# The first half of the latent branch moved ahead of the last pair's weighting

## The chip, the cores and the metric

One core of one Trainium2 chip. The metric is the device time of one launch in microseconds; lower is better. The program computes two transformer layers for 256 tokens, with weights that are read from HBM in each run.

## The reference, cut to what matters

Each layer runs three token mixers side by side on the same normalized input, projects each mixer's output to the model width, gates the three and adds them:

```python
y_a = einsum('bsk,kd->bsd', y_a, w_br_a)   # latent attention: 8 heads x 64 = 512 rows of weights
y_b = einsum('bsk,kd->bsd', y_b, w_br_b)   # block-sparse attention: 4 heads x 64 = 256 rows
y_c = einsum('bsk,kd->bsd', y_c, w_br_c)   # index-selected attention: 4 heads x 64 = 256 rows
g_a, g_b, g_c = split(sigmoid(gate_logits), 3)
merged = g_a * y_a + g_b * y_b + g_c * y_c
x = x + gate1 * (merged @ w_out)
...                                        # then SwiGLU, with its own norm
```

The projection of the latent attention (`y_a @ w_br_a`) is "the latent branch".

## The kernel before, in words

**Slabs.** All weights come as slabs of 128 partitions x up to 2048 words, numbered by their use, through a ring of three. For each slab SP issues a load into `raw` (it waits until the slab three before has been split), ACT rounds it into `w_hi` (`hi`, line 1006, which waits for the data and until TensorE has used the slab three before) and DVE subtracts for `w_lo` (`lo`, line 1377). TensorE then multiplies three times for each tile: hi x hi, hi x lo, lo x hi (`passes`, lines 543 to 545 in the helper's calls). `slab_used` counts the slabs that TensorE is done with.

**Attention.** Sixteen heads, in the order 4 of b, 8 of a (latent), 4 of c, run as a software pipeline that is written out by hand on each engine. On TensorE the loop `for n in range(NH + 4)` issues, per step, the scores of head n + 1, the transposes of head n - 3 (`turn_p`, line 819), every second step the weighting of a pair of heads (`weigh_v`, lines 837 and 841), and at eight of the steps half a slab of gate logits (`gate_slab`). The last steps are n = 18 (transposes of head 15, second half of gate slab 11) and n = 19 (`weigh_v(7)`, the last pair).

ACT copies the transposed weights out of PSUM (line 1271), then writes `y_hi` of a finished pair (line 1276, waits for `pv_done` of that pair). DVE writes `y_lo` of the pair (line 1708). `y_lo_done` counts the pairs; the latent heads are pairs 2 to 5, the c heads are pairs 6 and 7.

**After the attention.** For each half `hf` of the model width there are two slabs: `S_BR + 2 * hf` holds the latent branch (48 matmuls, "part a"), `S_BR + 2 * hf + 1` holds the b branch and the c branch (24 matmuls each, "part b" and "part c"). TensorE's order for half 0 is: part a (waits for `y_lo_done` of 6 pairs), eight transposes of a gate row (`turn_row`, line 575, wait for `gate_out`), part b, part c (waits for all 8 pairs). For half 1: part a (waits for the row copies, `row_out`), then a wait for `m_done` 2, part b, part c. Then the output projection `w_out`. Part b of half 1 writes the PSUM banks that DVE has to read for the merge of half 0; this is what `m_done` guards.

ACT's order there is: `y_hi` of pair 7, `hi` of slab `S_BR + 2`, `hi` of slab `S_BR + 3` (needs `slab_used` of `S_BR`, that is part a of half 0), two row copies (line 1055), `hi` of `S_OUT`, the rounding of the merged tiles (line 1296).

DVE's order there is: `lo` of `S_BR + 1`, `y_lo` of pair 7, `lo` of `S_BR + 2`, `lo` of `S_BR + 3`, then for half 0 two products of gate and latent branch (line 1734, need part a), two rounds of two products and two sums (lines 1745, 1749, 1750, need part c; the end of each round counts `m_done`), the low parts (line 1756), then `lo` of `S_OUT` and the same for half 1.

POOL waits for `pv_done` of the last pair before it issues the next three loads of adaLN weights (1 MB each) into buffers that the attention used.

Of the kernel before, what the change touches and what calls it, by code (L numbers as in the profile page):

```python
# [13 lines left out]
P = 128  # L14
D = 1024
T = 256
# [7 lines left out]
A_HEADS, A_NOPE, A_ROPE, A_QK, A_V = 8, 64, 32, 96, 64  # L24
Q_RANK, KV_RANK = 768, 256
B_HEADS = C_HEADS = 4
# [33 lines left out]
S_BR = S_GATE1 + 10  # L60
# [95 lines left out]
def gate_slab_no(g):  # L156

    return S_GATE0 + g if g < 2 else S_GATE1 + g - 2


def gate_bank(g):

    return 7 - g if g < 2 else (g + 1) % 3 if g < 6 else g - 5 if g < 8 else g % 2
# [18 lines left out]
NH = len(HEADS)  # L182
# [7 lines left out]
BR_BANKS = ((4, 6, 2), (0, 2, 4))  # L190
# [16 lines left out]
def build(nc, x, c, ada, slabs, vec, gain_rows, const, out):  # L207
    with ExitStack() as ctx:
        def sb(name, shape, dt=F32):
            return ctx.enter_context(nc.sbuf_tensor(name, shape, dt))  # L210

        def event(name, per_layer):
            return Event(ctx.enter_context(nc.semaphore(name)), per_layer)
# [8 lines left out]
        y_hi = sb("y_hi", [P, KT, T], F32R)  # L222
        y_lo = sb("y_lo", [P, KT, T], F32R)
# [83 lines left out]
        bank = [ctx.enter_context(nc.psum_tensor(f"bank{i}", [P, 512], F32)) for i in range(8)]  # L307
# [16 lines left out]
        slab_used = event("slab_used", NS)  # L324
# [27 lines left out]
        row_out = event("row_out", 4)  # L352
# [43 lines left out]
        y_lo_done = event("y_lo_done", NH // 2)  # L396
# [125 lines left out]
        def _(pe):  # L522
# [14 lines left out]
            def slab(l, s):  # L537
                pe.wait_ge(lo_ready.sem, lo_ready.at(l, s + 1))
                return (l * NS + s) % RING
# [7 lines left out]
            def channel_tile(slot, o, col, offs, act_hi, act_lo, opens, first, final):  # L547

                for n, off in enumerate(offs):
                    last = passes(o, w_hi[:, slot, off + col:off + col + P], w_lo[:, slot, off + col:off + col + P],  # L550
                                  act_hi[n], act_lo[n], first and opens and n == 0, final and n == len(offs) - 1)
                return last

            def channel_slab(slot, tiles, first, final):

                for o, col, offs, act_hi, act_lo, opens in tiles:
                    last = channel_tile(slot, o, col, offs, act_hi, act_lo, opens, first, final)
                return last
# [27 lines left out]
            def gate_slab(l, g, tiles=(0, 1)):  # L586

                s = gate_slab_no(g)
                slot = slab(l, s)
                if g >= 5:  # L590

                    pe.wait_ge(gate_out.sem, gate_out.at(l, g - 2 if g < 8 else g - 1))
                hi, lo = [h_hi[:, k, :] for k in range(KT)], [h_lo[:, k, :] for k in range(KT)]
                last = channel_slab(slot, [(bank[gate_bank(g)][:, m * T:(m + 1) * T], m * P,
                                            [256 * k for k in range(KT)], hi, lo, m == 0) for m in tiles], True, True)
                if 1 in tiles:
                    last.then_inc(slab_used.sem, 1)
# [20 lines left out]
            for l in range(DEPTH):  # L618
# [10 lines left out]
                if l == 0:  # L629
# [17 lines left out]
                    slot = (l * NS + S_A) % RING  # L647
# [51 lines left out]
                for k in range(KT):  # L699
                    slot = slab(l, S_B + k)  # L700
# [82 lines left out]
                for kind, src in ((0, q_a), (1, k_a)):  # L783
# [6 lines left out]
                    for h in range(A_HEADS):  # L790
                        for t in range(TT):
                            at = (h % 2) * T + t * P
                            m = (t * A_HEADS + h) * A_QK
# [4 lines left out]
                def scores(n):  # L798
                    kind, h = HEADS[n]
                    if kind == "a":  # L800
                        q, k = qk_t[0:A_QK, h, :], qk_t[0:A_QK, A_HEADS + h, :]
                    else:
                        j = (0 if kind == "c" else 1)
                        q, k = pq_t[:, 2 * j + h // 2, :], kz_t[:, 4 * j + h, :]
                    if n >= 2:

                        pe.wait_ge(ttr_done.sem, ttr_done.at(l, 2 * (n - 1)))
                    b = bank[4 + n % 2]
                    nc.tensor.matmul(b[:, 0:P], q[:, 0:P], k[:, 0:P], start=True, stop=True)
                    nc.tensor.matmul(b[:, P:P + T], q[:, P:T], k[:, :], start=True, stop=True).then_inc(scored.sem, 1)  # L810

                def turn_p(n):

                    pe.wait_ge(p_ready.sem, p_ready.at(l, n + 1))
                    if n >= 2:

                        pe.wait_ge(pt_out.sem, pt_out.at(l, n - 1))
                    for j in range(3):
                        last = nc.tensor.transpose(bank[6 + n % 2][:, j * P:(j + 1) * P],
                                                   p_sb[n % 5][:, j * P:(j + 1) * P], ident)  # L820
                    last.then_inc(p_tp.sem, 1)

                def weigh_v(pair):

                    if pair == 0:

                        pe.wait_ge(gate_out.sem, gate_out.at(l, 8))
                    if pair >= 2:

                        pe.wait_ge(y_lo_done.sem, y_lo_done.at(l, pair - 1))  # L830
                    pe.wait_ge(pt_out.sem, pt_out.at(l, 2 * pair + 2))
                    y, at = bank[2 + pair % 2], []
                    for n in (2 * pair, 2 * pair + 1):
                        kind, h = HEADS[n]
                        at.append({"a": P * h + A_NOPE, "b": C_BV + HD * h, "c": C_CV + HD * h}[kind])
                    for e in range(2):
                        nc.tensor.matmul(y[HD * e:HD * (e + 1), 0:T], proj[:, 0, at[e]:at[e] + HD],
                                         pt_sb[(2 * pair + e) % 3][:, 0:T], start=True, stop=False,
                                         skip_group_check=True)
                    for e in range(2):  # L840
                        nc.tensor.matmul(y[HD * e:HD * (e + 1), P:T], proj[:, 1, at[e]:at[e] + HD],
                                         pt_sb[(2 * pair + e) % 3][:, T:T + P], start=False, stop=True,
                                         skip_group_check=True).then_inc(pv_done.sem, 1)


                pe.wait_ge(mla_out_a.sem, mla_out_a.at(l, 4))
                scores(0)
# [3 lines left out]
                for n in range(NH + 4):  # L851
                    if 1 <= n < NH - 1:
                        scores(n + 1)
                    if 3 <= n <= NH + 2:
                        turn_p(n - 3)
                    if n >= 5 and n % 2:
                        weigh_v((n - 5) // 2)
                    if n in GATE_STEPS:
                        half = GATE_STEPS.index(n)
                        gate_slab(l, 8 + half // 2, (half % 2,))  # L860

                for hf in range(2):
                    banks = BR_BANKS[hf]

                    def branch(slot, b0, base, k0, n_k):
                        hi, lo = [y_hi[:, k0 + k, :] for k in range(n_k)], [y_lo[:, k0 + k, :] for k in range(n_k)]
                        return channel_slab(slot, [(bank[b0 + m // 2][:, (m % 2) * T:(m % 2 + 1) * T], m * P,
                                                    [base + 512 * k for k in range(n_k)], hi, lo, m % 2 == 0)
                                                   for m in range(4)], True, True)

                    s = S_BR + 2 * hf

                    pe.wait_ge(y_lo_done.sem, y_lo_done.at(l, (B_HEADS + A_HEADS) // 2))
                    if hf:
                        pe.wait_ge(row_out.sem, row_out.at(l, 2))
                    slot = slab(l, s)
                    branch(slot, banks[0], 0, 0, 4).then_inc(slab_used.sem, 1)
                    if hf == 0:

                        pe.wait_ge(gate_out.sem, gate_out.at(l, 12))  # L880
                        for half in range(2):
                            turn_row(l, 0, half, bank[half])
                    slot = slab(l, s + 1)
                    if hf:

                        pe.wait_ge(m_done.sem, m_done.at(l, 2))
                    branch(slot, banks[1], 0, 4, 2)
                    pe.wait_ge(y_lo_done.sem, y_lo_done.at(l, NH // 2))
                    branch(slot, banks[2], 1024, 6, 2).then_inc(slab_used.sem, 1)
# [1015 lines left out]
```

## Time and profile before

| | |
|---|---|
| median of 3 runs | 904.38 us (903.04 to 905.41) |
| the profiled execution's own time | 903.48 us |
| its span in the trace | 901.3 us |
| TensorE busy | 872.8 us, 97% of the span |
| DVE busy | 678.5 us, 75% |
| ACT busy | 498.1 us, 55% |
| chain that ended last | PE 68%, DVE 21%, ACT 4%, DMA 4%, issue 3% |

How to read it: the span is the time from the first to the last instruction in the trace; the device time holds 2.2 us more around it. A row of the timeline has the start, the duration, the engine, the line of the code, the operation with its output and inputs, the count and, in brackets, how long the engine had been idle before and what released it. Matmuls overlap each other, so their starts tell the pace and not their durations.

### The profile page before, as it was taken

The numbers are of one execution on the slowest core, as the hardware profiler recorded it, in microseconds if no ns is written. First come the engines' busy times: TensorE is split into PE (matmuls) and PEld (weight loads), VectorE is DVE, ScalarE is ACT, GpSimd is POOL, SyncE is SP. The second block draws the span as 40 slices with busy tenths as digits, with TensorE's granted clock in tenths as the row PEclk, the third lists the DMA queues.
The fourth block names the chain that finished last, engine by engine and source line by source line (L and its number), as shares of the span: only waits on it lengthen the run. The fifth ranks groups of instructions, "written<-read, shape, count | busy, mean of one in ns | idle before, by whom it ended". The sixth has DMA issues, their size and how long they took to land.

```text
span 901.3 us, 12713 instructions
## 1 busy us (share of the span) xinstructions
PE 872.8 (97%) x5012; PEld 752.1 (83%) x5012; DVE 678.5 (75%) x1065; ACT 498.1 (55%) x724; POOL 28.1 (3%) x52
## 2 busy tenths in 40 slices
PE   8998999998999999999989999999899999999998
PEld 5888979987977888888868999998798778888886
DVE  6987999897797765774679968998769755763544
ACT  6555788465466434443473468955654844434431
POOL 1010000000000000000001100000000000000000
PEclk9999999999999999999999999999999999999999
DMA  9979835343645776787538974451264366555441
GB/s 373 425 305 393 305 121 191 137 172 133 257 187 185 282 263 250 262 309 270 202 124 345 372 269 157 146 212 70 94 280 148 140 229 232 188 185 187 166 161 47
DMA packets 29580, 197.72 MB, mean 219 GB/s; under 512 B 3537, under 2 KB 3793, under 8 KB 7506
## 3 DMA queue, kind: packets, MB, share of 16 engines
q1 hardware_dynamic: 23474, 154.83, 45.9%
q0 software_dynamic: 5760, 41.95, 12.4%
q8 instruction: 40, 0.66, 0.3%
q10 hardware_dynamic: 288, 0.15, 0.1%
q14 instruction: 18, 0.15, 0.0%
HBM read 195.86 MB, written 1.05 MB: 218 GB/s over the span
## 4 chain that ended last, share of the span: by engine, by line
PE 68%; DVE 21%; ACT 4%; DMA 4%; issue 3%; DVEq 0%; ACTq 0%; POOLq 0%
PE bank L582 14%; PE bank L584 14%; PE bank L583 14%; DVE w_lo L1377 8%; PE bank L543 5%; PE bank L545 5%; PE bank L544 5%; DMA raw<-in_slabs_dram 3%; DVE front L1384 2%; ACT w_hi L1006 2%; DVE score L1569 1%; PE bank L941 1%; DVE acc L1688 1%; DMA front<-in_ada_dram 1%; DVE x_t L1429 1%
## 5 line engine op out<-in xcount | busy, mean ns | idle before, releaser
L1377 DVE TENSOR_TENSOR w_lo<-raw,w_hi 128x2048 fp32r<-128x2048 f32 (+2 forms) x146 | 316.8, 2172 | 131.4 <-ACT w_hi L1006 129.8
L1006 ACT ACTIVATE w_hi<-raw 128x2048 fp32r<-128x2048 f32 (+2 forms) x146 | 264.2, 1810 | 150.3 <-PE bank L584 92.3
L582 PE MATMUL bank<-w_hi,h_hi 128*128 128x512 f32 x536 | 211.3, 394 | 7.5 <-DVE w_lo L1377 5.1
L584 PE MATMUL bank<-w_lo,h_hi 128*128 128x512 f32 x536 | 209.2, 390 | 0.0
L583 PE MATMUL bank<-w_hi,h_lo 128*128 128x512 f32 x536 | 208.9, 390 | 0.0
L582 PEld LDWEIGHTS bank<-w_hi,h_hi 128*128 128x128 f32 x536 | 100.6, 188 | 33.8 <-DVE w_lo L1377 7.0
L584 PEld LDWEIGHTS bank<-w_lo,h_hi 128*128 128x128 f32 x536 | 100.6, 188 | 21.4
L583 PEld LDWEIGHTS bank<-w_hi,h_lo 128*128 128x128 f32 x536 | 100.7, 188 | 20.2
L543 PE MATMUL bank<-h_hi,w_hi 128*128 128x256 f32 x384 | 111.6, 291 | 3.1 <-DVE w_lo L1377 3.0
L545 PE MATMUL bank<-h_hi,w_lo 128*128 128x256 f32 x384 | 108.6, 283 | 0.0
L544 PE MATMUL bank<-h_lo,w_hi 128*128 128x256 f32 x384 | 108.5, 283 | 0.0
L1384 DVE CUSTOM_DVE_ANT_0 front<-front,cond,cols 128x1024 f32<-128x1024 f32 x68 | 85.3, 1291 | 5.1 <-DMA front<-in_ada_dram 5.1
L543 PEld LDWEIGHTS bank<-h_hi,w_hi 128*128 128x128 f32 x384 | 73.5, 191 | 5.2 <-issue 4.2
L544 PEld LDWEIGHTS bank<-h_lo,w_hi 128*128 128x128 f32 x384 | 73.6, 192 | 0.1
L545 PEld LDWEIGHTS bank<-h_hi,w_lo 128*128 128x128 f32 x384 | 73.5, 191 | 0.0
L582 PE MATMUL bank<-w_hi,y_hi 128*128 128x512 f32 x176 | 71.3, 405 | 0.0
L583 PE MATMUL bank<-w_hi,y_lo 128*128 128x512 f32 x176 | 69.5, 395 | 0.0
L584 PE MATMUL bank<-w_lo,y_hi 128*128 128x512 f32 x176 | 69.4, 394 | 0.0
L1321 ACT ACTIVATE proj<-bank 128x256 f32<-128x256 f32 x44 | 16.9, 384 | 76.7 <-PE bank L584 76.6
L1256 ACT ACTIVATE acc<-acc,small 128x128 f32<-128x128 f32 x64 | 28.6, 449 | 29.5 <-DVE small L1688 29.5
L584 PEld LDWEIGHTS bank<-w_lo,y_hi 128*128 128x128 f32 x176 | 33.2, 189 | 7.8
L583 PEld LDWEIGHTS bank<-w_hi,y_lo 128*128 128x128 f32 x176 | 33.3, 189 | 6.8
(201 smaller groups left out, 1262.9 us busy)
## 6 DMA issues: line engine op xcount, KB each, us to landing
raw<-in_slabs_dram SPq DMA_DIRECT2D x124, 1024.0 KB, 4.9
front<-in_ada_dram POOLq DMA_DIRECT2D x29, 1024.0 KB, 6.6
acc<-in_ada_dram POOLq DMA_DIRECT2D x11, 1024.0 KB, 8.4
raw<-in_slabs_dram SPq DMA_DIRECT2D x16, 552.0 KB, 7.5
front<-in_ada_dram SPq DMA_DIRECT2D x5, 1024.0 KB, 12.3
raw<-in_slabs_dram SPq DMA_DIRECT2D x6, 768.0 KB, 6.7
proj<-in_ada_dram SPq DMA_DIRECT2D x2, 1024.0 KB, 12.2
x_t<-in_x_dram SPq DMA_DIRECT2D x2, 512.0 KB, 4.3
```

The source lines that it names most:

```text
L543: nc.tensor.matmul(b_out, st_hi, mv_hi, start=start, stop=False, skip_group_check=True)
L544: nc.tensor.matmul(b_out, st_hi, mv_lo, start=False, stop=False, skip_group_check=True)
L545: return nc.tensor.matmul(b_out, st_lo, mv_hi, start=False, stop=stop, skip_group_check=True)
L582: nc.tensor.matmul(o, hh, wh, start=first, stop=False)
L583: nc.tensor.matmul(o, hl, wh, start=False, stop=False)
L584: return nc.tensor.matmul(o, hh, wl, start=False, stop=final)
L941: last = nc.tensor.transpose(bank[6][:, f * T + t * P:f * T + (t + 1) * P], glu[t][:, f * P:(f + 1) * P], ident)
L1006: nc.scalar.activation(w_hi[:, n % RING, 0:w], raw[:, n % RING, 0:w], ACT.Copy).then_inc(hi_ready.sem, 1)
L1256: nc.scalar.activation(p_sb[n % 5][:, c0:c1], p_sb[n % 5][:, c0:c1], ACT.Exp, bias=negmax[n % 3][:, t:t + 1], scale=-1.0, accum_out=rowsum ...
L1321: nc.scalar.activation(silu_g[n % 2], bank[4 + t][:, 0:256], ACT.Silu).then_inc(silu_done.sem, 1)
L1377: nc.vector.tensor_tensor(w_lo[:, n % RING, 0:w], raw[:, n % RING, 0:w], w_hi[:, n % RING, 0:w], ALU.subtract).then_inc(lo_ready.sem, 1)
L1384: ins = nc.vector.tensor_tensor_reduce(w, w, cond[:], 1.0, cols[:, l, col:col + 1], ALU.mult, ALU.add, mod[:, l, col:col + 1])
```

## The change

On TensorE, part a of half 0 (48 matmuls with its two waits) is taken from behind the attention loop and issued inside it, at n = 18, behind the last head's transposes and the second half of gate slab 11, and ahead of `weigh_v(7)` of n = 19. Part a of half 1 stays where it was. The helper `branch` moves up so that both can use it. No instruction is added or removed, and no other engine's program is changed.

```diff
+                def branch(slot, b0, base, k0, n_k):
+                    hi, lo = ...
+                    return channel_slab(slot, ...)
+
+                def first_branch(hf):
+                    pe.wait_ge(y_lo_done.sem, y_lo_done.at(l, (B_HEADS + A_HEADS) // 2))
+                    if hf:
+                        pe.wait_ge(row_out.sem, row_out.at(l, 2))
+                    branch(slab(l, S_BR + 2 * hf), BR_BANKS[hf][0], 0, 0, 4).then_inc(slab_used.sem, 1)
...
                     if n in GATE_STEPS:
                         half = GATE_STEPS.index(n)
                         gate_slab(l, 8 + half // 2, (half % 2,))
+                    if n == NH + 2:
+                        first_branch(0)
 
                 for hf in range(2):
                     banks = BR_BANKS[hf]
-                    def branch(slot, b0, base, k0, n_k):
...
                     s = S_BR + 2 * hf
-                    pe.wait_ge(y_lo_done.sem, y_lo_done.at(l, (B_HEADS + A_HEADS) // 2))
                     if hf:
-                        pe.wait_ge(row_out.sem, row_out.at(l, 2))
-                    slot = slab(l, s)
-                    branch(slot, banks[0], 0, 0, 4).then_inc(slab_used.sem, 1)
+                        first_branch(1)
```

## Rows read from the trace of the kernel before

**Rows 1.** The page: TensorE's busy time, its granted clock in 40 slices, transfers.
```profile
PE 872.8 (97%) x5012; PEld 752.1 (83%) x5012; DVE 678.5 (75%) x1065; ACT 498.1 (55%) x724; POOL 28.1 (3%) x52
...
PEclk9999999999999999999999999999999999999999
...
DMA packets 29580, 197.72 MB, mean 219 GB/s; under 512 B 3537, under 2 KB 3793, under 8 KB 7506
```

**Rows 2.** Timeline of TensorE, layer 0, around the last weighting (start us, us).
```profile
218.22 0.28 PE L545 MATMUL bank<-h_hi,w_lo 128*128 128x256 f32 x1
218.43 0.65 PE L837 MATMUL bank<-acc,proj 128*64 128x256 f32 x4
...
219.23 0.39 PE L543 MATMUL bank<-y_hi,w_hi 128*128 128x256 f32 x1
...
224.92 0.28 PE L545 MATMUL bank<-y_hi,w_lo 128*128 128x256 f32 x1
225.04 1.03 PE L575 MATMUL bank<-konst,row 128*128 128x128 f32 x8
```

**Rows 3.** Timeline of ACT, layer 0, the same stretch.
```profile
215.66 0.50 ACT L1271 ACTIVATE acc<-bank 128x384 f32<-128x384 f32 x1 [0.79 <-PE bank L819]
...
219.37 0.38 ACT L1276 ACTIVATE y_hi<-bank 128x256 fp32r<-128x256 f32 x1 [0.24 <-PE bank L841]
219.65 1.91 ACT L1006 ACTIVATE w_hi<-raw 128x2048 fp32r<-128x2048 f32 x1
225.30 1.91 ACT L1006 ACTIVATE w_hi<-raw 128x2048 fp32r<-128x2048 f32 x1 [3.74 <-PE bank L545]
227.12 1.07 ACT L1055 ACTIVATE row<-bank 128x512 f32<-128x512 f32 x2
```

**Rows 4.** Timeline of DVE, layer 0, from slab S_BR's low part to the merge's end.
```profile
206.83 2.29 DVE L1377 TENSOR_TENSOR w_lo<-raw,w_hi 128x2048 fp32r<-128x2048 f32 x1 [1.34 <-ACT w_hi L1006]
...
214.32 0.42 DVE L1708 TENSOR_TENSOR y_lo<-bank,y_hi 128x256 fp32r<-128x256 f32 x1
...
221.59 2.29 DVE L1377 TENSOR_TENSOR w_lo<-raw,w_hi 128x2048 fp32r<-128x2048 f32 x1 [0.70 <-ACT w_hi L1006]
227.25 2.29 DVE L1377 TENSOR_TENSOR w_lo<-raw,w_hi 128x2048 fp32r<-128x2048 f32 x1 [3.36 <-ACT w_hi L1006]
229.46 1.28 DVE L1734 SCALAR_TENSOR_TENSOR proj<-proj,bank 128x512 f32<-128x512 f32 x2
231.88 0.69 DVE L1745 SCALAR_TENSOR_TENSOR proj<-proj,bank 128x512 f32<-128x512 f32 x1 [1.14 <-PE bank L545]
...
236.57 0.69 DVE L1750 TENSOR_TENSOR proj<-proj,front 128x512 f32<-128x512 f32 x1
```

**Rows 5.** Timeline of TensorE: part a of half 1, first and last, and part b.
```profile
231.61 0.28 PE L543 MATMUL bank<-y_hi,w_hi 128*128 128x256 f32 x1
...
237.19 0.28 PE L545 MATMUL bank<-y_hi,w_lo 128*128 128x256 f32 x1
237.41 0.36 PE L543 MATMUL bank<-y_hi,w_hi 128*128 128x256 f32 x1
```

**Rows 6.** Timeline of DVE in half 1, layer 0.
```profile
243.44 1.28 DVE L1745 SCALAR_TENSOR_TENSOR front<-front,bank 128x512 f32<-128x512 f32 x2 [1.40 <-PE bank L545]
...
246.10 2.29 DVE L1377 TENSOR_TENSOR w_lo<-raw,w_hi 128x2048 fp32r<-128x2048 f32 x1
```

**Rows 7.** Timelines of ACT, DVE and TensorE: the same three places in layer 1.
```profile
658.57 0.38 ACT L1276 ACTIVATE y_hi<-bank 128x256 fp32r<-128x256 f32 x1 [0.24 <-PE bank L841]
...
671.07 0.69 DVE L1745 SCALAR_TENSOR_TENSOR proj<-proj,bank 128x512 f32<-128x512 f32 x1 [1.14 <-PE bank L545]
...
676.60 0.36 PE L543 MATMUL bank<-y_hi,w_hi 128*128 128x256 f32 x1
```

**Rows 8.** Timeline of POOL: its loads behind the last weighting.
```profile
219.63 1.05 POOL L479 DMA_DIRECT2D front<-in_ada_dram  x2 [24.29 <-PE bank L841]
```

**Rows 9.** Busy time by stretch: window, length, PE, PEld, DVE, ACT, POOL, PEclk, DMA share, GB/s.
```profile
268.00:272.00 4.00, 2.64 (x12) 1.89 (x11) 3.96 (x6) 3.43 (x11) 0.00 (x0) 1.00 0.00 0
```

More of the change, by code:

```diff
@@ L843, in weigh_v @@
                                          skip_group_check=True).then_inc(pv_done.sem, 1)
+                def branch(slot, b0, base, k0, n_k):
+                    hi, lo = [y_hi[:, k0 + k, :] for k in range(n_k)], [y_lo[:, k0 + k, :] for k in range(n_k)]
+                    return channel_slab(slot, [(bank[b0 + m // 2][:, (m % 2) * T:(m % 2 + 1) * T], m * P,
+                                                [base + 512 * k for k in range(n_k)], hi, lo, m % 2 == 0)
+                                               for m in range(4)], True, True)
+                def first_branch(hf):
[3 more added lines that the diff above has]
+                    branch(slab(l, S_BR + 2 * hf), BR_BANKS[hf][0], 0, 0, 4).then_inc(slab_used.sem, 1)
                 pe.wait_ge(mla_out_a.sem, mla_out_a.at(l, 4))
@@ L860, in _ @@
                         gate_slab(l, 8 + half // 2, (half % 2,))
+                    if n == NH + 2:
+                        first_branch(0)
                 for hf in range(2):
                     banks = BR_BANKS[hf]
-                    def branch(slot, b0, base, k0, n_k):
[L866 to L869, printed above, removed]
                     s = S_BR + 2 * hf
-                    pe.wait_ge(y_lo_done.sem, y_lo_done.at(l, (B_HEADS + A_HEADS) // 2))
                     if hf:
-                        pe.wait_ge(row_out.sem, row_out.at(l, 2))
-                    slot = slab(l, s)
-                    branch(slot, banks[0], 0, 0, 4).then_inc(slab_used.sem, 1)
+                        first_branch(1)
                     if hf == 0:
```

## The prediction

> **What bounds the kernel now.** I began with the page. TensorE is busy for 97% of the span, at a granted clock that never leaves the top level in any of the 40 slices [rows 1]. So a change can only help if it closes a gap of TensorE, and it hurts if it opens one. Next I read TensorE's timeline around the place of the edit, to see which gap the edit could close. The last matmul of the gate slab starts at 218.22, the last weighting at 218.43, part a of half 0 at 219.23 and its last matmul at 224.92, the row transposes at 225.04 [rows 2]. In a running stream one matmul of 256 columns follows another every 0.12 us (part a of half 1 starts its 48 matmuls from 231.61 to 237.19 [rows 5], 5.58 / 47 = 0.119). Between gate slab and weighting there is 0.21, so at most 0.09 us is lost there. The wait that a filler would hide, the copy of the last transposed head on ACT, ran at 215.66 and ended at 216.16 [rows 3], two microseconds ahead of the weighting: the half gate slab hides it already.
>
> Then I read what hangs on the last weighting, on the engines that work in order. On ACT, `y_hi` of pair 7 starts at 219.37, 0.94 after the weighting began, and slab S_BR + 2 is rounded right behind it, at 219.65; S_BR + 3 only at 225.30, after an idle time of 3.74 that ends with part a; the row copies at 227.12 [rows 3]. On DVE the low parts of these two slabs start at 221.59 and 227.25 (idle 3.36 before), the first products at 229.46, the merge at 231.88 (idle 1.14 before, for part c), and its last sum at 236.57 ends at 237.26 [rows 4]. Last, I looked at who waits for that. TensorE's part b of half 1 starts at 237.41, 0.22 after the matmul before it at 237.19 [rows 5], where the pace is 0.12: the merge of half 0 is already the last thing to come, by 0.10 us. It has no slack.
>
> **The change part by part.** *TensorE's own work.* The same instructions run in another order. Part a needs slab S_BR (its low part was done at 206.83 + 2.29 = 209.12) and six pairs (the sixth `y_lo` ended at 214.32 + 0.42 = 214.74) [rows 4]; both are there at 218.34, when it can start. So neither wait holds. Its last matmul then starts at 218.34 + 47 x 0.119 = 223.93, the weighting at + 0.21 = 224.14, and the transposes at + 0.80 (219.23 - 218.43) = 224.94, against 225.04 [rows 2]. By itself that is a gain of 0.10 us in each layer. Where it isn't held elsewhere it would be kept.
>
> *The weighting.* It comes 224.14 - 218.43 = 5.71 us later. A bound from below is 47 steps of 0.119 = 5.59; from above the whole stretch from 219.23 to 225.04, 5.81. I take 5.71, worked out from the starts themselves.
>
> *What is queued behind it on ACT.* `y_hi` of pair 7 now waits until 224.14 + 0.94 = 225.08. Slab S_BR + 2 is ready to be rounded since the gate slab ended, but it stands behind that wait: 225.08 + 0.28 = 225.36 in place of 219.65. S_BR + 3 follows at once, 225.36 + 1.82 = 227.18 (1.82 = 227.12 - 225.30, one rounding to the next start) in place of 225.30, since its own condition, part a, is met by then. The row copies start at 229.00 and end at 230.07. They are needed for part a of half 1 at 231.61 - 0.10 = 231.51 [rows 5]: 1.4 us to spare.
>
> *On DVE.* The low part of S_BR + 2 starts 1.94 after its rounding (221.59 - 219.65): 227.30. It ends at 229.59, before 231.51, with 1.9 to spare. The low part of S_BR + 3 starts 2.21 later (229.46 - 227.25), at 229.51; its input, rounded from 227.18, would allow 229.12. First products at 229.51 + 2.21 = 231.72. The merge starts behind these, 1.28 + 0.04 later (the chained step, by the gap between 243.44 + 1.28 [rows 6] and its follower), at 233.04. It started at 231.88. So of 5.71 us of delay, DVE's idle times take up 3.46 and 1.10, and 233.04 - 231.88 = 1.16 us come through. `y_lo` of pair 7 needs DVE from about 225.5 to 225.9 and TensorE wants it for part c at about 228.6; no wait there.
>
> *What waits for DVE.* From the merge's start to TensorE's part b of half 1 it is 237.41 - 231.88 = 5.53 us, of which nothing is shortened. Part b starts at 233.04 + 5.53 = 238.57 in place of 237.41: +1.16 us. TensorE's gain of 0.10 ahead of that is swallowed by the longer wait. Bounds: with 5.59 to 5.81 for the shift, 1.04 to 1.26.
>
> *Whether the loss is given back.* DVE waits 1.40 us for TensorE's part c of half 1 at 243.44 [rows 6], and from there the chain of the end runs on DVE. Both engines are late by the same 1.16, so that this idle time doesn't absorb it. All later waits I looked at are between TensorE, DVE and ACT and move together. *Transfers:* POOL's three loads of 1 MB go out when the weighting is done, at 219.63 + 5.7 = 225.3 [rows 8]. The load of slab S_OUT + 1 goes out when the low part of S_BR + 2 ends, near 229.6, and its low part is wanted at 246.10 + 1.16 = 247.26 [rows 6]. I cost it at nothing: over 15 us cover it.
>
> *Sum.* Layer 1 has the same three places at the same distances: 671.07 - 658.57 = 12.50 and 676.60 - 671.07 = 5.53 [rows 7], as in layer 0. So 2 x 1.16 = +2.3 us on the profiled execution's 903.48 (span 901.3 and 2.2 around it): 905.8. That execution lies 0.9 under the median of 904.38; on the median it is **906.7 us**, slower by 0.26%.
>
> **The rivals.** *Nothing comes through (904.2).* TensorE keeps the 0.10 us in each layer, 904.38 - 0.2. It needs DVE to have 1.2 us that I don't see. For it: TensorE's gap at the merge wait is just 0.10 us, and such a gap may also be a switch between streams. Against it: even then DVE ends the merge over a microsecond after TensorE arrives. This is the one that isn't slower; it decides if the merge starts before about 231.9.
>
> *The transfers collide (914.5).* POOL's loads now start close to the load of slab S_OUT + 1. If the five megabyte transfers (three of POOL's, two slabs, 5.24 MB) moved at the mean of 219 GB/s [rows 1], they would last 23.9 us from 225.3, to 249.2; the rounding must start by 247.26 - 1.94 = 245.3. That is 3.9 late in each layer, 904.38 + 2 x (1.16 + 3.9) = 914.5. For it speaks only that mean, which is one of a queue that often idles. The Trainium skill speaks against the change here: "Trainium Kernel Development and Optimization", Key Constraints, says that transfers from the different issuing engines all run on the same 16 DMA engines. No row here separates the two kinds.
>
> *The clock drops (912.4).* The new stop of TensorE is 238.57 - 237.20, less the one matmul's tail, about 1.1 us. If the granted clock fell from 2.4 to 1.2 GHz behind it, part b of half 1 (24 matmuls, 2.86 us) would take twice that: 2 x (1.16 + 2.86) = +8.0. Against it: in the stretch from 268 to 272 TensorE is busy for only 2.64 of 4.00 us, and the granted clock reads 1.00 [rows 9]. The Trainium skill, "TensorE: Matmul & The Clock Gate", Why this matters for your kernels, warns of idle gaps between bursts of matmuls for this reason; by that rule the stop would have to be long, and this case's row shows none of that at a longer one.
>
> **How the numbers follow.** Chances: the forecast 0.80, nothing comes through 0.12, transfers 0.05, clock 0.03. The bounds of the forecast (1.04 to 1.26 in each layer) give 906.5 to 906.9. The runs of before spread by 1.3 below and 1.0 above their median; this carries it to 905.2 and 907.9, and another such set of runs may lie as far off. With part of the first rival the range is 904.8 to 908.4. A measurement of this kernel can tell about 0.3% from no change, 901.67 and 907.09. The forecast lies 0.4 under the upper bound, so that about a third of its chance falls above: slower 0.8 x 0.34 + 0.08 = 0.35; faster 0.03, from the first rival's spread; the same 0.62.
>
> **What would show it.** In the changed kernel's trace: the last weighting near 224.1; `y_hi` of pair 7 near 225.1 with S_BR + 2 and S_BR + 3 rounded back to back behind it; no idle time on DVE between the low part of S_BR + 3 and the merge, which starts near 233.0 without a wait for TensorE; and ahead of part b of half 1 a stop of TensorE of about 1.1 us, released by DVE line 1750, in both layers. The prediction is wrong if the merge still waits for TensorE, if that stop isn't there, or if a wait for a slab's data stands anywhere between there and `w_out`.

## The result and the profile after

| | before | changed |
|---|---|---|
| median | 904.56 us (22 runs) | 906.20 us (22 runs) |
| lowest to highest | 902.52 to 908.72 | 904.84 to 907.19 |
| ratio, 95% interval | | 1.0019 (1.0011 to 1.0027) |
| profiled execution: span | 901.3 us | 902.9 us |
| TensorE / DVE / ACT busy | 872.8 / 678.5 / 498.1 us | 872.4 / 678.7 / 498.1 us |

The kernel became slower by 1.64 us (906.20 - 904.56), between 1.0 and 2.4 by the interval. The forecast was 906.7 us, +2.3. Here and below the ratio is taken over all executions, so it isn't quite the quotient of the two medians.

No engine has more work to speak of (DVE's busy time is 0.2 us longer, TensorE's 0.4 shorter). The difference lies in one place of each layer. First TensorE's timeline of the changed kernel in layer 0, which answers [rows 2] and [rows 5] (start us, us, then engine, line, operation; in brackets the idle time before and its releaser):

```profile
217.72 0.28 PE L545 MATMUL bank<-h_hi,w_lo 128*128 128x256 f32 x1
217.84 0.28 PE L543 MATMUL bank<-y_hi,w_hi 128*128 128x256 f32 x1
...
223.42 0.28 PE L545 MATMUL bank<-y_hi,w_lo 128*128 128x256 f32 x1
223.63 0.65 PE L837 MATMUL bank<-acc,proj 128*64 128x256 f32 x4
224.11 0.39 PE L841 MATMUL bank<-acc,proj 128*64 128x128 f32 x4
224.43 1.09 PE L575 MATMUL bank<-konst,row 128*128 128x128 f32 x8
...
238.05 0.36 PE L543 MATMUL bank<-y_hi,w_hi 128*128 128x256 f32 x1 [1.13 <-DVE proj L1757]
```

This execution arrives 0.50 us earlier at the gate slab's end (217.72, was 218.22), through earlier waits that differ from execution to execution (one stop of TensorE near 88 us took 1.84 us there and 1.24 here). So I count from there. Part a follows at + 0.12 without a wait, the weighting starts at + 5.91 (was + 0.21), the row transposes at + 6.71 (was + 6.82). Up to here TensorE is 0.11 us ahead; 0.06 of this is gone again at part b of half 0, which starts 0.85 behind the transposes' start in place of 0.79. Then, ahead of part b of half 1, stands a stop of 1.13 us that wasn't there, released by the merge's last sum (line 1757 now, 1750 before). Part b starts at + 20.33; before it was 237.41 - 218.22 = + 19.19. That is +1.14 us. Layer 1 has the same row, 20.33 behind its own gate slab:

```profile
678.31 0.36 PE L543 MATMUL bank<-y_hi,w_hi 128*128 128x256 f32 x1 [1.13 <-DVE proj L1757]
```

ACT's timeline, layer 0, answers [rows 3]:

```profile
218.04 0.60 ACT L1068 ACTIVATE front<-bank 128x512 f32<-128x512 f32 x1 [0.31 <-PE bank L545]
224.57 0.38 ACT L1283 ACTIVATE y_hi<-bank 128x256 fp32r<-128x256 f32 x1 [5.93 <-PE bank L841]
224.85 3.72 ACT L1013 ACTIVATE w_hi<-raw 128x2048 fp32r<-128x2048 f32 x2
228.47 1.07 ACT L1062 ACTIVATE row<-bank 128x512 f32<-128x512 f32 x2
```

ACT stands still for 5.93 us at `y_hi` of pair 7, and behind it two slabs are rounded back to back. In the kernel before ACT stood there for 0.24 us only. DVE, layer 0, answers [rows 4]:

```profile
224.99 0.42 DVE L1715 TENSOR_TENSOR y_lo<-bank,y_hi 128x256 fp32r<-128x256 f32 x1 [4.94 <-ACT y_hi L1283]
226.80 4.50 DVE L1384 TENSOR_TENSOR w_lo<-raw,w_hi 128x2048 fp32r<-128x2048 f32 x2 [1.38 <-ACT w_hi L1013]
231.21 1.28 DVE L1741 SCALAR_TENSOR_TENSOR proj<-proj,bank 128x512 f32<-128x512 f32 x2
232.52 0.69 DVE L1752 SCALAR_TENSOR_TENSOR proj<-proj,bank 128x512 f32<-128x512 f32 x1
```

The two idle times that DVE had, 3.36 before the low part of S_BR + 3 and 1.14 before the merge, are gone; its row for the merge has no bracket any more. The merge starts at + 14.80 (232.52 - 217.72) where it started at + 13.66.

The two traces also show that the loss isn't given back between the layers. At the gate slab of layer 0 the changed kernel is 0.50 us ahead of the one before, at part b of half 1 it is 0.64 behind (238.05 against 237.41), at layer 1's gate slab 0.57 behind (657.98 against 657.41), and at layer 1's part b 1.71 behind (678.31 against 676.60).

### The profile page after: what moved, and what is told of

Its sections match the earlier page's. It is cut to its first block, busy times and chain, and to the rows that moved or that the text cites. A ratio compares the mean times of both kernels' runs of the same rounds, so it can differ in the third digit from the quotient of the medians.

```text
span 902.9 us, 12713 instructions
## 1 busy us (share of the span) xinstructions
PE 872.4 (97%) x5012; PEld 751.9 (83%) x5012; DVE 678.7 (75%) x1065; ACT 498.1 (55%) x724; POOL 28.3 (3%) x52
## 3 DMA queue, kind: packets, MB, share of 16 engines
HBM read 195.86 MB, written 1.05 MB: 218 GB/s over the span
## 4 chain that ended last, share of the span: by engine, by line
PE 65%; DVE 23%; ACT 5%; DMA 4%; issue 3%; SPq 0%; DVEq 0%; ACTq 0%
PE bank L582 14%; PE bank L584 14%; PE bank L583 14%; DVE w_lo L1384 9%; PE bank L543 5%; PE bank L544 5%; PE bank L545 5%; DMA raw<-in_slabs_dram 3%; ACT w_hi L1013 2%; DVE front L1391 2%; DVE score L1576 1%; PE bank L948 1%; DVE acc L1695 1%; DVE x_t L1436 1%; PE bank L710 1%
```

## The experiments

Three theories. **Q**, the queue: ACT's wait for the late weighting holds back the rounding of S_BR + 2, DVE's merge becomes late and TensorE stops. **D**, the transfers: POOL's loads go out later and collide. **O**, the order: TensorE's own sequence costs the time. Each run stands beside runs of the kernel before on the same chip. In the table "weighting", "merge" and "part b" are the starts in layer 0, counted from the start of the gate slab's last matmul. Only one execution of each run has a trace; the ratio is over all of them.

| run | weighting | merge | part b | ratio (95%) | median, before beside it |
|---|---|---|---|---|---|
| before | 0.21 | 13.66 | 19.19 | | |
| r1 changed | 5.91 | 14.80 | 20.32 | 1.0021 (1.0009 to 1.0033) | 905.86, 904.13 |
| r2 queue open | 5.91 | 13.61 | 19.14 | 1.0008 (0.9998 to 1.0018) | 904.32, 904.13 |
| r3 before, late rounding | 0.21 | 14.69 | 20.22 | 1.0021 (1.0010 to 1.0032) | 905.85, 904.13 |
| r4 three tiles ahead | 4.48 | 13.65 | 19.18 | 1.0001 (0.9987 to 1.0014) | 903.51, 904.13 |
| r5 rows ahead too | 6.79 | 15.68 | 21.21 | 1.0074 (1.0060 to 1.0087) | 910.00, 903.48 |
| r6 before, POOL late | 0.20 | 13.65 | 19.18 | 1.0000 (0.9989 to 1.0010) | 903.44, 903.48 |
| r7 merge order | 0.21 | 13.66 | 19.19 | 0.9991 (0.9983 to 1.0000) | 902.03, 903.48 |
| r8 queue open, merge order | 5.91 | 13.61 | 19.13 | 0.9989 (0.9981 to 0.9998) | 902.86, 903.48 |
| r9 rows ahead again | 6.78 | 15.67 | 21.20 | 1.0073 (1.0056 to 1.0091) | 910.75, 903.83 |
| r10 rows ahead, stop filled | 6.79 | 15.68 | 21.12 | 1.0039 (1.0027 to 1.0051) | 907.47, 903.83 |
| r11 changed, stop filled | 5.91 | 14.80 | 20.24 | 1.0027 (1.0018 to 1.0037) | 905.86, 903.83 |
| r12 merge order again | 0.21 | 13.66 | 19.19 | 0.9976 (0.9966 to 0.9985) | 901.66, 903.83 |

**r1, the changed kernel again.**

> The changed kernel once more, beside the three variants of this call. Theory Q (the queue behind the last weighting: ACT's wait for it holds back the rounding of slab S_BR + 2, so DVE's merge of half 0 is late by what its idle times don't take up): +1.15 us in each layer, 1.5 to 2.4 us over the kernel before in all. Theory D (POOL's loads go out 5.2 us later and collide with a slab load) and theory O (TensorE's own order costs the time) say the same of this run; it is the mark for the others.

It measured +1.73 us, the stop again 1.13 us in layer 0 and 1.12 in layer 1.

**r2, the queue opened.** TensorE and POOL as in the changed kernel.

```diff
 # ACT, n = NH + 4
+                    if n == NH + 4:
+                        hi(l, S_BR + 2)
                     if n >= 6 and n % 2 == 0:
                         ...                                  # y_hi of the pair
 # DVE, n = NH + 5
+                    if n == NH + 5:
+                        lo(l, S_BR + 2)
                     if n >= 7 and n % 2:
                         ...                                  # y_lo of the pair
 # ACT and DVE, behind the attention: the two calls leave their old places
-                        hi(l, S_BR + 2)
...
-                        lo(l, S_BR + 2)
```

> The changed kernel, with slab S_BR + 2 taken out of the queue behind the last weighting: ACT rounds it ahead of y_hi of pair 7, DVE takes its low part ahead of y_lo of pair 7. TensorE and POOL are as in the changed kernel. Theory Q: DVE's merge waits for TensorE's part c again, no stop of TensorE ahead of part b of half 1; the loss of 1.6 us is gone and 0.1 us a layer is kept, -0.2 us against the kernel before (-0.5 to +0.3). Theories D and O: the loss stays, +1.6 us.

DVE's timeline of r2, layer 0:

```profile
221.22 2.29 DVE L1385 TENSOR_TENSOR w_lo<-raw,w_hi 128x2048 fp32r<-128x2048 f32 x1 [0.42 <-ACT w_hi L1013]
225.73 0.42 DVE L1718 TENSOR_TENSOR y_lo<-bank,y_hi 128x256 fp32r<-128x256 f32 x1 [2.22 <-ACT y_hi L1285]
227.53 2.29 DVE L1385 TENSOR_TENSOR w_lo<-raw,w_hi 128x2048 fp32r<-128x2048 f32 x1 [1.38 <-ACT w_hi L1013]
229.74 1.28 DVE L1743 SCALAR_TENSOR_TENSOR proj<-proj,bank 128x512 f32<-128x512 f32 x2
232.07 0.69 DVE L1754 SCALAR_TENSOR_TENSOR proj<-proj,bank 128x512 f32<-128x512 f32 x1 [1.05 <-PE bank L545]
```

The merge waits for TensorE again (1.05 us) and part b starts at + 19.14: the loss in the trace is gone although the weighting is as late as in the changed kernel. The median is 0.2 us over the one beside it; the interval holds no change, and not r1's 1.0021. The two intervals overlap, so it is the trace that decides here. The gain of 0.2 us that was expected doesn't show. Of the 0.11 us that TensorE gains at the row transposes 0.06 is gone at part b of half 0, so that 0.05 arrives at part c's end and, 5.53 us of DVE later, at part b of half 1. The result is for Q and against D and O, since POOL's loads and TensorE's order are those of the changed kernel.

**r3, the late rounding alone.** The kernel before, with one wait on ACT.

```diff
                     if hf == 0:
+                        act.wait_ge(slab_used.sem, slab_used.at(l, S_BR + 1))
                         hi(l, S_BR + 2)
```

> The kernel before, TensorE and POOL unchanged; ACT only waits for slab_used of S_BR (end of part a) ahead of the rounding of S_BR + 2, so that this starts at about 225.3 in place of 219.65, as in the changed kernel. Theory Q: the merge starts about 1.1 us late, TensorE stops about 1.0 us (released by DVE line 1750) in each layer, +2.2 us on the kernel before (+1.5 to +2.5). Theories D and O: no change, 0 +- 0.4 us.

ACT's timeline of r3 in layer 0, then TensorE's:

```profile
219.26 0.38 ACT L1276 ACTIVATE y_hi<-bank 128x256 fp32r<-128x256 f32 x1 [0.24 <-PE bank L841]
225.13 3.72 ACT L1006 ACTIVATE w_hi<-raw 128x2048 fp32r<-128x2048 f32 x2 [5.48 <-PE bank L545]
```

```profile
238.33 0.36 PE L543 MATMUL bank<-y_hi,w_hi 128*128 128x256 f32 x1 [0.97 <-DVE proj L1751]
```

`y_hi` isn't late here, only the rounding is, and TensorE's order is that of before. The stop is there (0.97 us), part b is 1.03 late, and the time is that of the changed kernel (1.0021). So the rounding's delay is enough by itself.

**r4, three of four tiles ahead.**

```diff
-                        first_branch(0)
+                        first_branch(0, (0, 1, 2))
...
+                    else:
+                        first_branch(0, (3,))
```

The helper takes the tiles as an argument, and the slab counts as used with the last of them.

> The changed kernel, but only three of part a's four tiles (36 matmuls) go ahead of the last weighting, the fourth behind it. The weighting is late by 36 x 0.119 = 4.3 us. Theory Q has a threshold: DVE's idle times take up 3.46 + 1.10 = 4.56 us, so nothing comes through: merge at about 231.6 would be ready 0.2 us before part c, 0 against the kernel before (-0.3 to +0.4). Theory D and theory O have none: three quarters of the loss, +1.2 us.

ACT rounds both slabs back to back here too, from 223.85. But DVE's row for the merge is

```profile
231.79 0.69 DVE L1756 SCALAR_TENSOR_TENSOR proj<-proj,bank 128x512 f32<-128x512 f32 x1 [0.32 <-PE bank L545]
```

so 0.32 us of idle time is left of the 1.14, and part b starts at + 19.18. The weighting is late by 4.27 us and nothing comes through. The sum has a threshold, the 3.46 + 1.10 = 4.56 us that DVE's idle times take up; it lies between this dose and the full one, 5.70, and what is left of the idle time, 0.32, is what the sum leaves (4.56 - 4.27 = 0.29).

**r5, the row transposes ahead as well.**

```diff
                         first_branch(0)
+                        pe.wait_ge(gate_out.sem, gate_out.at(l, 12))
+                        for half in range(2):
+                            turn_row(l, 0, half, bank[half])
...
-                        pe.wait_ge(gate_out.sem, gate_out.at(l, 12))
-                        for half in range(2):
-                            turn_row(l, 0, half, bank[half])
```

> The changed kernel with the eight row transposes (0.79 us) ahead of the last weighting as well: the weighting is late by 5.7 + 0.8 = 6.5 us. Theory Q: beyond the threshold every further microsecond comes through whole: merge 1.94 us late, stop of TensorE about 1.9 us in each layer, +3.9 us on the kernel before by the sum, +3.2 if scaled by what the changed kernel measured (1.64 for 2.3). Theory D (in proportion to POOL's delay) 1.64 x 6.5 / 5.7 = +1.9 us; theory O +1.6 us.

In the trace the slope is as said: weighting 0.88 later than in the changed kernel, merge 0.88 later, part b 0.88 later (21.21), a stop of 1.97 us. Two layers give 2 x (21.21 - 19.19) = +4.0. But the kernel measured +6.5 us. The rest is the granted clock, as the trace of r5 and then r9 and r10 show. Busy time by stretch in layer 1 (window, length, PE, PEld, DVE, ACT, POOL, PEclk, DMA share, GB/s):

```profile
678.00:682.00 4.00, 2.04 (x17) 1.86 (x16) 3.90 (x7) 1.11 (x2) 0.00 (x0) 0.97 1.00 424
682.00:686.00 4.00, 4.00 (x24) 4.00 (x23) 3.90 (x5) 2.07 (x2) 0.00 (x0) 0.60 0.19 80
```

The same second stretch of the kernel before:

```profile
682.00:686.00 4.00, 4.00 (x21) 3.38 (x20) 3.29 (x5) 2.50 (x2) 0.00 (x0) 1.00 0.52 215
```

and TensorE's timeline of r5 across the stop:

```profile
679.40 0.28 PE L545 MATMUL bank<-y_hi,w_lo 128*128 128x256 f32 x1
681.63 0.41 PE L543 MATMUL bank<-y_hi,w_hi 128*128 128x256 f32 x1 [1.96 <-DVE proj L1755]
681.84 0.41 PE L544 MATMUL bank<-y_lo,w_hi 128*128 128x256 f32 x1
...
685.24 0.29 PE L545 MATMUL bank<-y_hi,w_lo 128*128 128x256 f32 x1
685.36 0.28 PE L543 MATMUL bank<-y_hi,w_hi 128*128 128x256 f32 x1
```

Behind the stop 17 matmuls come 0.21 us apart (681.63 to 685.24) and the next ones 0.12 apart: the clock is at its lower level, 1.2 GHz, and then at 2.4 again. That costs 3.61 - 17 x 0.119 = 1.6 us for one such fall. The trace of r5 has a second one from 650.87 to 654.5, behind a stop of 1.90 us in the attention. That stop isn't r5's: the kernel before has it too, and so has every run, once in each layer. First its row in the kernel before and the stretch behind it, then the same two of r5:

```profile
648.54 0.65 PE L837 MATMUL bank<-acc,proj 128*64 128x256 f32 x4 [1.90 <-ACT acc L1271]
651.00:655.00 4.00, 3.66 (x33) 3.19 (x32) 1.24 (x5) 1.29 (x4) 0.00 (x0) 1.00 0.50 209
```

```profile
650.07 0.65 PE L837 MATMUL bank<-acc,proj 128*64 128x256 f32 x4 [1.90 <-ACT acc L1276]
651.00:655.00 4.00, 4.00 (x22) 4.00 (x23) 2.27 (x12) 1.36 (x5) 0.00 (x0) 0.57 0.76 262
```

**r6, POOL's loads late, alone.** The kernel before, with one wait on POOL.

```diff
                 pool.wait_ge(pv_done.sem, pv_done.at(l, NH))
+                pool.wait_ge(slab_used.sem, slab_used.at(l, S_BR + 1))
```

> The kernel before, in which POOL alone waits for the end of part a ahead of its three loads, so that they go out at about 225.3 in place of 219.6. Theory Q: nothing waits for these loads or for the slab loads beside them: 0 +- 0.4 us on the kernel before. Theory D: the whole loss or more, +1.6 us and up. Theory O: 0.

POOL's row:

```profile
225.45 1.05 POOL L479 DMA_DIRECT2D front<-in_ada_dram  x2 [30.42 <-PE bank L546]
```

The loads go out 7.53 us behind the gate slab's end (225.45 - 217.92), which was 1.41 in [rows 8] and is 7.12 in the changed kernel. Part b stays at + 19.18, the ratio is 1.0000. POOL's loads alone cost nothing, and r3 has the whole loss with these loads as early as before. D is out.

**r7 and r12, another order in the merge of half 1.** The rows of before showed DVE idle for 1.40 us and then, between the two rounds of the merge, a low part of 2.2 us on the chain that ends last [rows 6]. The low part goes into the idle time:

```diff
                     dve.wait_ge(m_first.sem, m_first.at(l, 2 * hf + 2))
+                    if hf:
+                        lo(l, S_OUT + 1)
...
-                        if hf and q == 0:
-                            lo(l, S_OUT + 1)
```

> The kernel before with one other place for DVE's low part of slab S_OUT + 1 in half 1: ahead of the merge, where DVE sits idle for 1.40 us, and no longer between its two rounds. The first round starts 0.85 us later, the second round, the low parts of the merged tiles and of S_OUT + 2 and S_OUT + 3 about 1.35 us earlier. TensorE's stop of 0.55 us at 254.77 for the low part of S_OUT + 3 should close: -0.55 us in each layer, -1.1 us (-2.0 to 0). If TensorE is bound there by its own stream, nothing or up to -0.3. If the first merged quarter, 0.85 us later, is wanted at once, slower by up to +0.8 us in each layer.

> The kernel of r7 (low part of S_OUT + 1 ahead of the merge of half 1) once more, because its interval reached to no change: -1.1 to -1.5 us on the kernel before if the gain is real, 0 if it was chance.

DVE's timeline of r7, layer 0:

```profile
240.60 1.28 DVE L1734 SCALAR_TENSOR_TENSOR proj<-proj,bank 128x512 f32<-128x512 f32 x2
241.91 2.29 DVE L1377 TENSOR_TENSOR w_lo<-raw,w_hi 128x2048 fp32r<-128x2048 f32 x1
244.12 1.28 DVE L1747 SCALAR_TENSOR_TENSOR front<-front,bank 128x512 f32<-128x512 f32 x2
245.44 0.69 DVE L1751 TENSOR_TENSOR proj<-proj,front 128x512 f32<-128x512 f32 x1
```

The idle time is gone, and TensorE has no stop between 243 and 262 in either trace, where before it had one of 0.55 us. r7 gained 1.45 us, r12 on another chip 2.17. The interval of r12 (0.9966 to 0.9985) lies clear of no change, where r7's just reaches it. The forecast was 1.1 to 1.5, so r12 gained more than the stop of 0.55 us in each layer explains; where the rest comes from stays open.

**r8, both.** r2's and r7's edits together.

> The changed kernel with the queue opened (S_BR + 2 rounded ahead of y_hi of pair 7 on ACT, its low part ahead of y_lo of pair 7 on DVE) and the low part of S_OUT + 1 ahead of the merge of half 1. Theory Q: the two add, -0.2 - 1.1 = -1.3 us on the kernel before (-2.2 to 0), the fastest of all. By theories D and O the loss of 1.6 us stays: +0.5 us.

It is 0.1% below the kernel before (0.9989) and no faster than r7 (902.86 against 902.03), so it isn't the fastest of all, as was forecast: the opened queue takes the loss away and adds nothing that can be measured.

**r9 to r11: is the rest of r5 the clock?** r9 is r5's kernel again; r10 fills its stop, r11 that of the changed kernel (with 2 in place of 4):

```diff
                     if hf:
+                        pe.wait_ge(m_first.sem, m_first.at(l, 2))
+                        for _ in range(4):
+                            nc.tensor.matmul(bank[4][:, 0:T], kz_t[:, 0, 0:P], kz_t[:, 0, :], start=True, stop=True)
                         pe.wait_ge(m_done.sem, m_done.at(l, 2))
```

> The kernel of r5 (rows ahead of the last weighting too) once more, as the mark for the next one: it measured +6.5 us where the sum of its two stops of 1.97 us gives +4.0. Theory C: the rest is the granted clock, which in r5's trace fell to half behind such a stop. Then it shows again +6 us with a mean clock under 0.998 in most executions. If the extra was chance of one chip: +4 us.

> The kernel of r9, with four unused matmuls of 0.39 us (zeros, into a bank that is free there) in the stop ahead of part b of half 1. They don't shorten DVE's merge, so the stop of 1.97 us is filled to about 0.4 but part b starts no earlier: +4.0 us by the sum stays. Theory C (the clock falls behind the stop of TensorE): the extra 2.5 us goes, +4 us (3.4 to 4.8), mean clock up to that of the kernel before. If the extra has another source, it stays at +6 us.

> The changed kernel, with two such unused matmuls in its stop of 1.13 us. Part b starts no earlier. If the stop of 1.13 us costs clock as well, it is faster than the changed kernel by up to 0.5 us; if it doesn't, both are equal at +1.7 to 2.3 us on the kernel before.

r9 repeats r5: +6.9 us, mean clock 0.998 or lower in 5 of 6 executions. Its one execution at a mean clock of 1.000 took 907.07 us. Its profiled one took 909.23 and has a single fall, behind the stop of 1.95 us in layer 1. r10 has the merge at the same place (15.68), part b 0.08 earlier, more instructions than r9, and is 3.3 us faster (907.47 against 910.75); its mean clock was 0.999 or 1.000 in all 5 executions. All of these (906.88 to 907.74) lie where r9 lies without a fall. The expectation calls the unused operand zeros; by the kernel only half of its partitions are, the others hold keys of the attention. TensorE's row (the trace counts the four matmuls as eight) in the filled stop, and the stretch that had 0.60 in r5:

```profile
237.20 1.89 PE L892 MATMUL bank<-kz_t 128*128 128x256 f32 x8
239.24 0.39 PE L543 MATMUL bank<-y_hi,w_hi 128*128 128x256 f32 x1
```

```profile
682.00:686.00 4.00, 4.00 (x36) 4.00 (x36) 3.62 (x4) 1.44 (x1) 0.00 (x0) 1.00 0.14 35
```

Its +3.6 us agrees with the sum of the two late starts, 2 x (21.12 - 19.19) = 3.9. r11 has the changed kernel's own time, 905.86: a stop of 1.13 us, filled or not, makes no difference that these runs can tell.

## Why the prediction was right, point by point

- *TensorE's own work, -0.10 us:* measured -0.11 (transposes at + 6.71, was + 6.82). Neither of part a's waits held. That this gain would be kept where nothing else holds was half right: by r2 0.05 was left at part b of half 0.
- *The weighting 5.71 us later:* 5.91 - 0.21 = 5.70.
- *ACT's queue:* `y_hi` at + 6.85 (224.57 - 217.72), forecast 225.08 - 218.22 = 6.86. The two slabs back to back, as said. r3 shows this delay to be enough, r2 shows it to be needed.
- *DVE absorbs 3.46 and 1.10:* measured 3.46 and 1.11, since behind the gate slab the low part of S_BR + 2 starts 5.71 later, the first products 2.25 and the merge 1.14; the forecast of the last was 1.16. The prediction's own steps give 3.45 for the first (5.71 - 2.26), a slip of 0.01. r4 and r5 lie on the two sides of the threshold: 4.27 us late costs nothing, 6.58 us late costs 2.02.
- *Part b 1.16 late:* 1.14 in both layers, with a stop of 1.13, forecast 1.1.
- *Nothing given back, transfers covered:* the lead and lag of the two traces above give 1.14 in layer 0 and 1.14 in layer 1, and at most 0.07 back between them. DVE's idle time of 1.40 us in half 1 stayed (its row at 244.09 in the changed kernel), and r6 shows no price.
- *The sum:* 2 x 1.14 = 2.3 us by the traces. The two medians lie 1.64 and 1.73 us apart, and the intervals (1.0 to 2.4 and 0.8 to 3.0) hold 2.3. Some executions of both kernels have a fall of the clock or two in them and others none. Of those with a mean clock of 1.000, beside r1, the median was 902.95 before (14) and 905.02 changed (3), 2.1 apart. The 22 executions of the result can't be sorted like this, as those of the kernel before have no clock on record; the six changed ones at 1.000 have a median of 905.66. So the traces need no other term, and the difference between 1.6 and 2.3 is within the scatter. That it comes from falls of the clock isn't shown.
- *A third of the chance above +0.3%:* the measured ratio is +0.19%, its interval ends at 0.27%. The forecast of the change was 0.7 us high. The time itself came out only 0.5 high because the starting point, a median of three executions, lay 0.18 under that of the 22 (904.38, 904.56); that part is luck.
- *Rivals:* the first (nothing comes through) fell with the stop in the trace, the second with r6. The third, the clock, didn't happen in the changed kernel's trace, but I argued against it with one stretch, a stop of 1.36 us that left the clock at 1.00 [rows 9], as if this held for longer ones. A better row stood in the same trace: two stops of 1.90 us in the attention, longer than the forecast one, with the clock at 1.00 behind both. Even that would have been weak, since behind the same stops other traces have a fall. My price was too high as well: 2.86 us for a fall behind the stop, where r5 shows 1.6. r5, r9 and r10 show that with stops of 1.97 us the falls raise the cost of the move by more than half (+6.5 where the stops give +4.0). Had the move been 0.9 us longer, the forecast by the sum alone (+4.0) would have missed +6.5.

## What to carry to other kernels

Before work is put ahead of an instruction, look at who waits for that instruction on the other engines and what stands behind the waits in their queues: here the 5.7 us passed through ACT's `y_hi` to a rounding that had nothing to do with it. Add up the idle times along that path, since they are the budget of the move (4.6 us here, 36 matmuls but not 48), and look for the gap that the move should close before you pay for it: this one was at most 0.09 us. If a stop of TensorE comes out of it, price the clock behind it as well.

## What the runs showed of the hardware that I had not expected

- **One stop of about 2 us is enough for the lower clock level, sometimes.** Behind 1.96 us of idle time in layer 1 of r5 17 matmuls ran at 0.21 us a piece in place of 0.12, which cost 1.6 us. Behind the same stop in layer 0 of the same execution the clock stayed at 1.00, and r9's trace has it the same way, so it fell behind two of four such stops. Behind the two stops of 1.90 us in the attention it fell in 5 of 28 cases over the fourteen traces (r5 and r11 in layer 1, r8 in layer 0, r12 in both). Behind the stops of 1.0 to 1.85 us it fell in none, those of 1.13 us among them. By the rule in the Trainium skill, "TensorE: Matmul & The Clock Gate", Why this matters for your kernels, idle gaps between bursts of matmuls throw the clock back; the trace of r5 agrees, but with a shorter gap than the page names. What decides between a fall and none at the same stop isn't shown.
- **Much of this kernel's scatter goes with such falls.** Where the traces show one, it is mostly behind the two stops of 1.90 us that the kernel before has as well. Beside r1 the kernel before has a median of 902.95 us in its 14 executions at a mean clock of 1.000, 904.90 in the 11 at 0.998 and 905.17 in the 6 at 0.996. The trace of r12, with a fall in each layer's attention, took 903.87 us, and r12's six executions at 1.000 a median of 901.57. No execution of the kernel before beside any run (84) was under 0.996, but 5 of the 11 of r5 and r9 were at 0.994, so their longer stops add falls of their own. In r6's profiled execution, which came out at 907.84 us against a median of 903.44, the clock falls behind a stop of 3.03 us for a slab's low part in layer 1, far from the edit:

```profile
535.15 0.35 PE L544 MATMUL bank<-h_hi,w_hi 128*128 128x256 f32 x1 [3.03 <-DVE w_lo L1378]
...
535.64 0.41 PE L544 MATMUL bank<-h_hi,w_hi 128*128 128x256 f32 x1
535.85 0.41 PE L545 MATMUL bank<-h_lo,w_hi 128*128 128x256 f32 x1
```

- **Unused work can pay.** Four useless matmuls in each layer made r10 3.3 us faster than r9. The falls in the attention aren't r5's doing, since r8, r11 and r12 have them too without a stop of 1.97 us. By its mean clocks r10 had none of them, and with ten such stops in its five executions that may be chance. How much of the 3.3 us is from the filled stop of layer 0 and how much from that of layer 1 stays open.
